# Two attentions of a fused three-block kernel: scores issued two heads ahead, values one head behind

## Reference

```python
def mla_project(p, norm_q, norm_kv, w_q_up, w_kv_up, rope):      # 6 heads
    q = (rms_norm(q_lat, norm_q) @ w_q_up).reshape(B, N, 6, 128 + 64)
    kv = (rms_norm(kv_lat, norm_kv) @ w_kv_up).reshape(B, N, 6, 128 + 128)
    ...                                  # the 64 rope columns of q and k are rotated
def attend(q, k, v):
    s = einsum('bqhd,bkhd->bhqk', q, k) * scale
    pr = softmax(s)
    return einsum('bhqk,bkhd->bqhd', pr, v)

def diff_attention(h, w_qkv, lam, subln_g, w_o, cos, sin, layer_idx):   # 8 heads
    sc = einsum('bqhcd,bkhcd->bhcqk', q, k)       # c = 0, 1: two score maps a head
    p = softmax(sc)
    a = p[:, :, 0] - lam_full * p[:, :, 1]
    o = einsum('bhqk,bkhe->bqhe', a, v)
    return (rms_norm_3(o, subln_g) * (1 - lam_init)).reshape(b, s, d) @ w_o
```

## Time and profile before

| | |
|---|---|
| median of 3 runs | 2965.69 us (2962.95 to 2967.80) |
| the profiled execution | 2967.82 us, its span in the trace 2966.3 us |
| TensorE (PE) busy | 2641.4 us, 89% of the span |
| VectorE (DVE) busy | 779.6 us, 26% |
| ScalarE (ACT) busy | 345.6 us, 12% |
| mean granted TensorE clock | 0.931 of full speed |

### The profile page before, as it was taken

One profiled execution on the slowest core, in us unless ns is written; L12 is line 12 of the kernel. 1 busy time (PEld: TensorE's weight loads), 2 busy tenths in 40 slices (PEclk: granted clock), 3 DMA queues, 4 the chain that ended last, 5 costly groups with the idle time before them and its releaser, 6 DMA issues. The chain is left out here.

```text
span 2966.3 us, 28580 instructions
## 1 busy us (share of the span) xinstructions
PE 2641.4 (89%) x10835; PEld 1557.5 (53%) x10836; DVE 779.6 (26%) x1776; ACT 345.6 (12%) x678; POOL 43.2 (1%) x67
## 2 busy tenths in 40 slices
PE   6978599999999899978999889969998998957998
PEld 3433333333333233327877667737675776734775
DVE  1231322121212121224651333343641001242001
ACT  2111111111111111110122010020001001021000
POOL 0000000000000000000000010000000000000000
PEclk8977599999999899999989999989999999968999
DMA  7600499999998899988325268536985543120442
GB/s 304 248 0 0 180 418 428 429 428 428 428 429 347 341 429 428 428 358 300 132 104 198 100 224 308 207 132 233 331 322 199 170 143 104 57 85 5 152 150 98
DMA packets 187865, 727.06 MB, mean 245 GB/s; under 512 B 9743, under 2 KB 103277, under 8 KB 159141
## 3 DMA queue, kind: packets, MB, share of 16 engines
q1 hardware_dynamic: 168180, 650.26, 55.8%
q0 software_dynamic: 19632, 76.09, 6.6%
HBM read 725.27 MB, written 1.05 MB: 245 GB/s over the span
## 5 line engine op out<-in xcount | busy, mean ns | idle before, releaser
L2152 PE MATMUL bank<-hT,big 128*128 128x256 f32 x2816 | 623.3, 383 | 14.7 <-DMA big<-in_ffn_w_gu 8.8
L2152 PEld LDWEIGHTS bank<-hT,big 128*128 128x128 f32 x2816 | 539.9, 192 | 108.9 <-issue 24.7
L1354 PE MATMUL bank<-experts_raw,tiled_xs 128*64 128x512 f32 x2112 | 474.4, 599 | 16.7 <-DMA experts_raw<-in_w_up 12.9
L1354 PEld LDWEIGHTS bank<-experts_raw,tiled_xs 128*64 128x64 f32 x2112 | 147.9, 138 | 332.7 <-issue 295.4
L2166 PE MATMUL bank<-big,ffn_actT 128*128 128x512 f32 x704 | 309.1, 592 | 1.5 <-ACT third_gate L2238 1.5
L1354 PE MATMUL bank<-experts_raw,tiled_act_s 128*64 128x512 f32 x1056 | 241.2, 603 | 48.3 <-DMA experts_raw<-in_w_down 47.0
L1683 PE MATMUL bank<-hT,ring 128*128 128x256 f32 x1024 | 224.3, 382 | 3.8 <-DMA ring<-in_w_in 2.7
L2166 PEld LDWEIGHTS bank<-big,ffn_actT 128*128 128x128 f32 x704 | 133.6, 190 | 153.2 <-issue 151.3
L2255 DVE TENSOR_TENSOR ffn_actT<-ffn_silu,bank 128x256 f32<-128x256 f32 x88 | 36.9, 421 | 672.9 <-ACT ffn_silu L2221 672.9
L1683 PEld LDWEIGHTS bank<-hT,ring 128*128 128x128 f32 x1024 | 196.5, 192 | 32.5 <-issue 5.7
L1354 PEld LDWEIGHTS bank<-experts_raw,tiled_act_s 128*64 128x64 f32 x1056 | 71.6, 138 | 195.9 <-issue 124.2
(11 more groups left out here) (468 smaller groups left out, 1932.1 us busy)
## 6 DMA issues: line engine op xcount, KB each, us to landing
experts_raw<-in_w_gate SPq DMA_DIRECT2D x64, 2048.0 KB, 23.7
experts_raw<-in_w_up SPq DMA_DIRECT2D x64, 2048.0 KB, 25.1
experts_raw<-in_w_down SPq DMA_DIRECT2D x64, 2048.0 KB, 25.5
big<-in_ffn_w_gu SPq DMA_DIRECT2D x88, 1024.0 KB, 9.8
ring<-in_mod_w POOLq DMA_DIRECT2D x30, 2048.0 KB, 11.9
big<-in_ffn_w_down SPq DMA_DIRECT2D x44, 1024.0 KB, 5.0
ring<-in_w_in SPq DMA_DIRECT2D x16, 2048.0 KB, 7.6
mla_wm<-in_w_mod SPq DMA_DIRECT2D x24, 1024.0 KB, 7.0
```

What stands on the lines that cost most here:

```text
L1354: last = nc.tensor.matmul(bank[b][h * HALF:(h + 1) * HALF, :], stationary(kt), raw[p][:, k, h * C:(h + 1) * C], start=kt == 0, stop=kt == ...
L2152: last = nc.tensor.matmul(bank[b][:, m * SEQ:(m + 1) * SEQ], wgu[:, s, m, k, f * P:(f + 1) * P], core.hT[:, k, :], start=k == 0, stop=k == ...
```

## The change

In the first attention `project` loses its last matmul to a function `turn(h)`, and `attend` is split in `turn_prob(h)` and `values(h)`. The heads now follow each other as project(h + 2), turn_prob(h), turn(h + 2), values(h - 1), scores(h + 2). The two query tiles of the turned probabilities go through banks 7 and 0 in place of 7 twice, ScalarE copies them (`take_turned`) in place of VectorE, and the values go into bank 1. VectorE's list becomes maxima(h + 1), rotate(h + 2), finish(h + 1), take_out(h - 1); ScalarE's keys(h + 2), exponents(h + 1), take_turned(h). In the differential attention the order becomes scores(h + 2), turn_prob(h), attend(h - 1); VectorE's finish(h), take_o(h - 2), maxima(h + 2); ScalarE's list stays. No arithmetic changes and no transfer.

```diff
                     last.then_inc(*core.filled[0].up())
+                    keys_at[h] = core.filled[0].sent
...
                     last.then_inc(*core.filled[1].up())
+
+                def turn(h):
                     pe.wait_ge(*qr_raw.next(pe))
                     core.claim(pe, 2)
                     nc.tensor.matmul(bank[2][0:ROPE, 0:SEQ], table("turn1")[0:ROPE, :], rot[:, 0, :],
...
-                    core.copied(pe, 0)
+                    pe.wait_ge(core.emptied[0].sem, keys_at[h])
...
-                def attend(h):
+                def turn_prob(h):
                     for t in range(TT):
+                        b = (7, 0)[t]
                         pe.wait_ge(*normed.next(pe))
-                        core.claim(pe, 7)
+                        core.claim(pe, b)
                         for c in range(2 * TT):
-                            last = nc.tensor.transpose(bank[7][:, c * P:(c + 1) * P],
+                            last = nc.tensor.transpose(bank[b][:, c * P:(c + 1) * P],
                                                        prob[h % 2][:, t, c * P:(c + 1) * P], core.ident[:])
-                        last.then_inc(*core.filled[7].up())
-                    core.copied(pe, 7)
-                    core.claim(pe, 2)
+                        last.then_inc(*core.filled[b].up())
+                        turned_at[h, b] = core.filled[b].sent
+
+                def values(h):
+                    for b in (7, 0):
+                        pe.wait_ge(core.emptied[b].sem, turned_at[h, b])
+                    core.claim(pe, 1)
                     for c in range(2 * TT):
-                        last = nc.tensor.matmul(bank[2][:, 0:SEQ], v[:, c, h * VDIM:(h + 1) * VDIM],
+                        last = nc.tensor.matmul(bank[1][:, 0:SEQ], v[:, c, h * VDIM:(h + 1) * VDIM],
                                                 probT[h % 2][:, c, :], start=c == 0, stop=c == 2 * TT - 1)
-                    last.then_inc(*core.filled[2].up())
+                    last.then_inc(*core.filled[1].up())
...
+                turn(0)
+                project(1)
                 scores(0)
                 gate_half(2, 0)
+                turn(1)
+                scores(1)
+                gate_half(2, 1)
                 for h in range(H_MLA):
-                    if h + 1 < H_MLA:
-                        project(h + 1)
-                        if h == 0:
-                            gate_half(2, 1)
-                        scores(h + 1)
-                    attend(h)
+                    if h + 2 < H_MLA:
+                        project(h + 2)
+                    turn_prob(h)
+                    if h + 2 < H_MLA:
+                        turn(h + 2)
+                    if h >= 1:
+                        values(h - 1)
+                    if h + 2 < H_MLA:
+                        scores(h + 2)
+                values(H_MLA - 1)
...
+                def take_turned(h):
+                    for t in range(TT):
+                        b = (7, 0)[t]
+                        act.wait_ge(*core.filled[b].next(act))
+                        nc.scalar.activation(probT[h % 2][:, :, t * P:(t + 1) * P],
+                                             bank[b][:].rearrange("p (c n) -> p c n", c=2 * TT), ACT.Copy)\
+                            .then_inc(*core.emptied[b].up())
...
             scores(0)
+            scores(1)
             for h in range(H3):
-                if h + 1 < H3:
-                    scores(h + 1)
-                attend(h)
+                if h + 2 < H3:
+                    scores(h + 2)
+                turn_prob(h)
+                if h:
+                    attend(h - 1)
+            attend(H3 - 1)
...
             maxima(0)
+            maxima(1)
             for h in range(H3):
-                if h + 1 < H3:
-                    maxima(h + 1)
                 finish(h)
+                if h >= 2:
+                    take_o(h - 2)
+                if h + 2 < H3:
+                    maxima(h + 2)
+            take_o(H3 - 2)
+            take_o(H3 - 1)
```

More of the change, by code:

```diff
@@ L797, in _ @@
                 last.then_inc(*core.filled[4].up())
+                keys_at, turned_at = {}, {}
                 def project(h):
@@ L851, in _ @@
                 turn_rows(pe, 2, 7)
+                turn(0)
+                project(1)
                 scores(0)
                 gate_half(2, 0)
+                turn(1)
+                scores(1)
+                gate_half(2, 1)
                 for h in range(H_MLA):
[L855 to L860 removed]
+                    if h + 2 < H_MLA:
[8 more added lines that the diff above has]
+                values(H_MLA - 1)
                 pe.wait_ge(*w_out_in.next(pe))
[L862 removed]
+                core.copied(pe, 1, 4)
                 for t in range(TT):
@@ L968, in finish, with take_out @@
                                                 ALU.mult).then_inc(*normed.up())
[L969 to L974, removed]
-                    nc.vector.tensor_copy(mixT[:, h, :], bank[2][:, 0:SEQ]).then_inc(*core.emptied[2].up())
+                def take_out(h):
+                    dve.wait_ge(*core.filled[1].next(dve))
+                    nc.vector.tensor_copy(mixT[:, h, :], bank[1][:, 0:SEQ]).then_inc(*core.emptied[1].up())
                 for b, n in ((3, 6), (4, 5), (5, 1), (6, 4)):
@@ L990, in _ @@
                     core.filled[b].passed(dve, 2)
+                rotate(1)
                 maxima(0)
+                finish(0)
                 for h in range(H_MLA):
                     if h + 1 < H_MLA:
-                        rotate(h + 1)
                         maxima(h + 1)
-                    finish(h)
+                    if h + 2 < H_MLA:
+                        rotate(h + 2)
+                    if h + 1 < H_MLA:
+                        finish(h + 1)
+                    if h >= 1:
+                        take_out(h - 1)
+                take_out(H_MLA - 1)
                 dve.wait_ge(*gain_in.next(dve))
@@ L1058, in exponents @@
                             .then_inc(*core.emptied[b].up())
+                def take_turned(h):
[5 more added lines that the diff above has]
+                            .then_inc(*core.emptied[b].up())
                 keys(0)
+                keys(1)
                 gate_row(2, 0)
                 exponents(0)
-                for h in range(1, H_MLA):
-                    keys(h)
-                    if h == 1:
-                        gate_row(2, 1)
-                    exponents(h)
+                gate_row(2, 1)
+                for h in range(H_MLA):
+                    if h + 2 < H_MLA:
+                        keys(h + 2)
+                    if h + 1 < H_MLA:
+                        exponents(h + 1)
+                    take_turned(h)
                 for b, n in ((3, 8), (4, 8), (5, 4), (6, 3)):
@@ L2480, in attend @@
                 last.then_inc(*core.filled[b].up())
-                core.copied(pe, b)
+            def attend(h):
+                core.copied(pe, 4 + h % 2)
                 b = 6 + h % 2
```

1 line of the change is left out of this document (added).

## The result

The changed kernel takes 2870.24 us (median of 4 runs, 2861.19 to 2877.25) against 2964.32 of the kernel before on the same chip (4 runs, 2961.48 to 2967.80): a ratio of 0.968, 95% interval 0.9645 to 0.9716, so 94 us faster. The forecast was 2894 with a range from 2872: the sign was right, and the gain was 24 us larger than forecast. The profiled execution is the longest of the four, 2877.25 us.

What follows compares the result with a forecast made beforehand. Both attention loops were taken as bound by chains of waits, with TensorE's low clock mattering as much. 2967.8 (profiled execution) - 41 - 31 = 2895.8; that execution being 2.1 above the median, 2894 us, range 2872 to 2934.

Steps and rivals of the forecast that it cites:

- neither bound but a mean clock of 0.80: First attention: clock assumed low for 40% of the time, between 3 us saved at low clock and 54 at full.
- upper bound: First attention at full clock throughout: 51.5 us saved up to the output projection, 2.9 more in it, 54 together.
- The term: First attention's predicted saving, about 41 us: 38.7 before the output projection and 1.8 in it.
- The differential term: Differential attention's predicted saving, 31 us of the 67.3 its eight heads took.
- the low-clock value: Differential attention with TensorE at its lower clock: 38 us against 67.3, 29 saved.
- The rival's bound by VectorE: Differential attention at full clock: VectorE, needing 3.9 us a head, sets the pace; 37 us saved.
- the clock stays high in both loops: Rival for both attentions: full clock saves 54 + 37 = 91 us, giving 2875 us; chance 0.2.
- the five stops of a head: First attention: TensorE's five waits of 0.51 to 1.57 us, together 4.7 us a head, should be gone.
- the 3.60 of the differential head: Differential attention: 3.60 us of each 9.49 us head, waiting for maxima, exponentials and normalisation, could be covered.
- the gain would be passed on past the barrier: Expert stage: its weights are first requested behind the barriers, so it starts earlier by what the first attention saves.
- The ring that closes again: Rival: ScalarE's turned copies wait for later scores, costing 3.3 us a first-attention head; 2980 us, chance 0.04.
- the gain swallowed by the expert stage: Rival: the expert weights' bandwidth sets the pace, so the first attention's gain is lost; 2935 us, chance 0.03.

Runs made afterwards that it cites:

- number 3: Kernel before, old order, with nine unused matmuls a head ahead of TensorE's waits in the first attention: 2929.32 us, ratio 0.9895 to the kernel before.
- number 1: Changed kernel with the differential attention put back to the order of before, new order in the first attention only: 2909.99 us, ratio 0.9828 to the kernel before.
- number 4: The changed kernel run once more, nothing edited, for a second profile: 2862.63 us, ratio 0.9674 to the kernel before.
- number 5: Changed kernel with both turned probability tiles of the first attention through bank 7 again: 2878.80 us, ratio 0.9722 to the kernel before.
- number 6: Changed kernel with each first-attention head's values made in the same turn, not one later: 2872.30 us, ratio 0.9694 to the kernel before.
- number 9: Changed kernel with each differential head's values made at once, scores still two heads ahead: 2870.36 us, ratio 0.9679 to the kernel before.
- number 10: Changed kernel with differential scores one head ahead in place of two, values still one behind: 2893.72 us, ratio 0.9770 to the kernel before.

## Why the prediction came out as it did

**The step that failed is the clock,** in both loops. For the first attention the prediction took "neither bound but a mean clock of 0.80", reasoning that narrow operations had stood before each fall of the clock. They mostly had, but so had stops, and number 3 parts the two: with the narrow operations in place and the stops filled, the clock is 1.00. The trace of before held a hint that the prediction read past. Ahead of the clock's first fall stood no row of narrow operations but wide score matmuls and a stop of 1.56; the granted clock was 1.00 from 155.2 to 155.5, when the first transposition had run for 0.13 us, and 0.50 from there to 162.3:

```profile
152.68 1.12 PE L830 MATMUL bank<-mla_heads_kr,mla_heads_qr 64*128 64x512 f32 x2
155.37 1.01 PE L838 MATMUL bank<-ident,mla_heads_prob 128*128 128x128 f32 x4 [1.56 <-DVE mla_heads_prob L967]
```

The price at full clock was right (12.6 a head forecast, 12.19 measured; upper bound 51.5 + 2.9, measured 53.0 + 2.6 in number 1). The term was put at 41 and measures 49 in the first profiled run of the changed kernel (46.5 + 2.6), with its slow stretch of 13.5 us, and 55.6 without. By the rule of the Trainium skill that the prediction cited (page "TensorE: Matmul & The Clock Gate", Part 1) the upper bound would hold. The traces without a slow stretch agree with it; that of the changed kernel does not for 13.5 us, in which TensorE was busy for 13.46 and stayed at 1.2 GHz.

**The differential term** was put at 31, "near the low-clock value, which rests on measured rows throughout". That the rows were measured was no reason that they would hold: they were measured under the stops that the change removes. The rival's bound by VectorE came true, 3.76 a head against 3.9 forecast, with 38.9 saved against 37. The clock did not have to be high throughout for that: it was 0.59 from 2553.7 to 2561 and 0.86 over the stage.

**The rival "the clock stays high in both loops"**, 2875 us at a chance of 0.2, was the case that happened. Its 91 us compare with 94 measured at first and 97 by the ratio of number 4; the two lengths and the projection give 94.5 where no slow stretch comes (53.0 + 38.9 + 2.6). The range's low end, 2872, left nothing for a sum slightly larger than this rival's, nor for the spread of some 10 us that the untouched stages bring; it should have reached to about 2860.

**What was right:** that the five stops of a head would go, and the 3.60 of the differential head (1.14 is left, at VectorE's pace); that nothing would bind but TensorE in the first loop and that ScalarE's list would hold (no stop for a ScalarE copy there in either trace of the changed kernel); the wait for head 2's queries and the one at the end; that the gain would be passed on past the barrier; the second bank's 0.8 a head, which number 5 measures as 0.96 in a middle head. The ring that closes again, and the gain swallowed by the expert stage, did not occur. **What was missed:** the wait for head 1's queries, which by the same reasoning as head 2's should have been on the list, since `turn(1)` stands directly ahead of `scores(1)`. It cost 0.96 us itself, and 6.5 more in the trace in which the clock stayed low for 13.5 us behind it.

**Which of the change's parts did it:** in the first attention the order that puts other matmuls ahead of each wait, and the second bank (8.5); not the delayed values (2) and not ScalarE (0.4). In the differential attention the scores two heads ahead (24.9 of 38.9 are lost without them), not the delayed values (2.5).

## What to carry to other kernels

In a loop in which TensorE stands still often and its granted clock is low, price the new order at the full clock as the likely case, if the experiment below says that the stops hold the clock down. Here they did: the clock alone was at least 26.3 of the 53.0 us that the first attention gave, and 15.5 of the 38.9 of the differential one. The experiment needs no pipelining: put unused matmuls in front of the waits; if the kernel gets faster by doing more, the clock was the price. Then check the first turns of the pipeline by hand, where the cover of the steady state is missing: one matmul moved behind `turn(1)` gave the shortest heads.

## What the runs showed of the hardware

- Nine unused matmuls a head made the first attention 26.3 us shorter (132.3 to 106.0), nine in the differential attention 15.5 (75.0 to 59.5), at a granted clock of 1.00 in both. Unfilled, stops of 0.5 to 1.6 us, 4.7 in a head of 23.75, went with a granted clock of 0.66.
- A stop by itself doesn't decide. One of 0.78 in each head of 13.15 us left the clock at 1.00 in number 5. One of 1.78 in its fifth head was followed by 3.4 us at 1.2 GHz, one of the same length in number 6 by none. The single stop of 0.96 ahead of head 1's scores was followed by 13.5 us at 1.2 GHz in the changed kernel's first trace, by 10.2 in number 9's, and by none in six others.
- Once low, dense work didn't bring the clock back at once: TensorE was busy 13.46 of 13.50 us at 0.52 before it rose, and all of the 10.20 us at 0.50 in number 9. What decides between the two outcomes stays open.
- TensorE busy 13.27 of 19.00 us was granted 0.91 in the new differential attention; busy 23.18 of 46.00 in number 10 it was granted 0.69, in this stretch of its heads:

```profile
2558.00:2604.00 46.00, 23.18 (x112) 19.43 (x112) 23.50 (x58) 16.49 (x49) 0.00 (x0) 0.69 0.00 0
```
